# Two-layer hybrid trunk on one core: fp32r sort of tokens, routing beside the first pass, down projection by halves

## What is computed

```
h = rms_norm(x) * gain
g_idx = argmax(softmax(h @ wg + bg))                  # one of 4 groups
e_p, e_idx = top2(softmax(expert logits of that group))  # 2 of its 4 experts
combine = one_hot(expert) * g_p * e_p / sum(e_p)
for e in range(16):
    a = silu(h @ w_gate[e]) * (h @ w_up[e])           # 2048 -> 512
    y += combine[:, e] * (a @ w_down[e])              # 512 -> 2048
x = x + y
```

## Time and profile before

| | us |
|---|---|
| three runs | 1616.9, 1619.32, 1620.0 |
| median | 1619.32 |
| the profiled execution | 1620.66 |
| its span on the engines | 1618.8 |

### The profile page before, as it was taken

How to read it: one execution, slowest core, us unless ns; L and a number is a source line. 1 busy time by engine, 2 the same in 40 slices (tenths; PEclk the granted TensorE clock), 3 DMA queues, 4 the chain that set the end, 5 groups by cost and what they waited for, 6 DMA issues and landing times.

```text
span 1618.8 us, 21643 instructions
## 1 busy us (share of the span) xinstructions
PE 1549.9 (96%) x7394; PEld 1272.5 (79%) x7394; DVE 1388.3 (86%) x1717; ACT 1076.6 (67%) x1286; POOL 11.7 (1%) x23
## 2 busy tenths in 40 slices
PE   5999989988999999999999996899999999999998
PEld 5998786466888888888888885688888888888886
DVE  3389987853799999999999996589999999999998
ACT  4344433053678877878787775478887787787785
POOL 0000000000000000000000000000000000000000
PEclk9999999989999999999999998999999999999999
DMA  8764533433499999999999992179999999999993
GB/s 270 241 208 131 160 128 104 156 142 145 189 380 379 359 350 381 377 339 378 373 353 348 388 348 112 34 287 373 382 358 366 374 377 336 378 376 345 368 373 134
DMA packets 100026, 469.29 MB, mean 290 GB/s; under 512 B 18810, under 2 KB 22220, under 8 KB 50548
## 3 DMA queue, kind: packets, MB, share of 16 engines
q1 hardware_dynamic: 98724, 466.85, 77.9%
q10 hardware_dynamic: 1232, 1.54, 0.3%
HBM read 466.24 MB, written 2.11 MB: 289 GB/s over the span
## 4 chain that ended last, share of the span: by engine, by line
PE 81%; DVE 12%; issue 4%; ACT 2%; DMA 0%; POOL 0%; DVEq 0%; SPq 0%; ACTq 0%; POOLq 0%
PE ps L1514 23%; PE ps L1516 23%; PE ps L1515 23%; DVE split_lo L953 5%; PE ps L1596 3%; PE ps L1803 2%; PE ps L1471 2%; PE ps L1817 1%; DVE cat L953 1%; DVE work L1068 1%; PE ps L1500 1%; ACT split_hi L610 1%; DVE split_lo L957 1%; DVE work L995 1%; DMA x_sb<-in_x 0%
## 5 line engine op out<-in xcount | busy, mean ns | idle before, releaser
L610 ACT ACTIVATE split_hi<-ring 128x1024 fp32r<-128x1024 f32 x856 | 903.6, 1059 | 310.1 <-PE ps L1516 294.2
L953 DVE TENSOR_TENSOR split_lo<-ring,split_hi 128x1024 fp32r<-128x1024 f32 x856 | 1023.0, 1220 | 100.6 <-ACT split_hi L610 70.1
L1514 PE MATMUL ps<-split_hi,cat 128*128 128x512 f32 (+1 forms) x1728 | 680.1, 394 | 8.2 <-DVE cat L953 7.2
L1516 PE MATMUL ps<-split_hi,cat 128*128 128x512 f32 (+1 forms) x1728 | 671.8, 389 | 0.0
L1515 PE MATMUL ps<-split_lo,cat 128*128 128x512 f32 (+1 forms) x1728 | 671.5, 389 | 0.0
L1514 PEld LDWEIGHTS ps<-split_hi,cat 128*128 128x128 f32 x1728 | 325.3, 188 | 82.8 <-issue 17.0
L1516 PEld LDWEIGHTS ps<-split_hi,cat 128*128 128x128 f32 x1728 | 324.9, 188 | 67.5
L1515 PEld LDWEIGHTS ps<-split_lo,cat 128*128 128x128 f32 x1728 | 325.3, 188 | 64.7 <-issue 0.5
L1514 PE MATMUL ps<-cat,split_hi 128*128 128x256 f32 x384 | 112.4, 293 | 11.4 <-DVE split_lo L953 11.4
L1515 PE MATMUL ps<-cat,split_hi 128*128 128x256 f32 x384 | 111.0, 289 | 0.0
L1516 PE MATMUL ps<-cat,split_lo 128*128 128x256 f32 x384 | 110.9, 289 | 0.0
(11 more groups left out here) (181 smaller groups left out, 669.5 us busy)
## 6 DMA issues: line engine op xcount, KB each, us to landing
ring<-in_w_gate SPq DMA_DIRECT2D x128, 1024.0 KB, 5.9
ring<-in_w_up SPq DMA_DIRECT2D x128, 1024.0 KB, 6.2
ring<-in_w_down SPq DMA_DIRECT2D x128, 1024.0 KB, 6.2
ring<-in_w_in_e SPq DMA_DIRECT2D x32, 1024.0 KB, 5.1
ring<-in_w_out_e SPq DMA_DIRECT2D x16, 1024.0 KB, 5.1
ring<-in_pool_w_o SPq DMA_DIRECT2D x4, 1024.0 KB, 8.4
x_sb<-in_x SPq DMA_DIRECT2D x4, 512.0 KB, 6.7
ring<-in_w_in_e SPq DMA_DIRECT2D x8, 256.0 KB, 5.0
```

The lines of the kernel that those rows point to most:

```text
L610: return nc.scalar.activation(out, in_, ACT.Copy, scale=scale)
L953: return tt(dst, full, hi.bitcast(F32), ALU.subtract)
L1514: mm(out, sh, mh, start=start, stop=False, **how)
L1516: return mm(out, sl, mh, start=False, stop=stop, **how)
```

## The change

- **Sort in fp32r.** x is split like a weight: ACT writes `x_parts[0]` (hi) per 512 channels (`hi_of_x`), DVE `x_parts[1]` (lo) (`lo_of_x`), in `cat`, the two token tiles interleaved (a step of 128 bytes between the channels of a group). The one-hot `sort_pick` holds bare ones, in `split_hi`'s slot 3. PE does first all 32 lo matmuls, then all 32 hi, into banks 0 to 7. ACT copies only the first 128 slots to `hgT` at once; `sorted_from(i)` fills `sorted_x` for bank 0 at once and for the others between the splits of the first pass. Unit 3 is split after all banks are sorted (before: ahead of the sort).
- **1/rms** is no longer in the one-hot. Its square is multiplied into the expert weights, and half of it is a fifth column of `comb_now` that the tanh takes as its scale; so `tanh(0)` and `gate(0)` come after the turned picks (unit 19) instead of after unit 10 to 12, in every pass.
- **Routing beside the first pass.** Expert choice, weights, windows and number of passes are cut into eight functions that DVE runs between its splits of units 4 to 15 of the first pass; register reads of the number of passes move behind the first pass on ACT, DVE and PE, the window's read to just before its use.
- **Down by halves.** `down(e)` goes through column halves outside, k inside; a down block is loaded as 2 chunks of k x 1024 columns (4 KB pieces instead of 8 KB).
- **act** is written contiguously by DVE; the transposes read it with a step of four elements.
- **Last pass** is a copy of its own: no slots for a next pass, `y_hi`/`y_lo` of banks 0 and 1 and their first scatters beside the last down; scatters in the order `SCATTER`.
- **Seam.** ACT splits pool units 0 to 2 before the last `y_hi`, DVE units 0 and 1 between its adds, 2 before and 3 after the sum of squares; units 4 to 7 after instead of before the second and fourth add.

```diff
+SCATTER = ((0, 0), (0, 1), (1, 0), (1, 1), (0, 2), (0, 3), (1, 2), (1, 3))
+BANKS_FIRST = {(0, "u"): 2, (1, "g"): 4, (0, "d"): 8}
+        x_parts = [cat[:, at:at + 2 * D].rearrange("p (c t) -> p t c", t=NT) for at in (2 * D, 0)]
+        sort_pick = split_hi[:, SPLITS - 1, 0:NT * 2 * P].rearrange("p (t s) -> p t s", t=NT)
...
+            if kind == "d":
+                half, pair = (j % 4) // 2, j % 2
+                w = a[name][l].rearrange("e (p k) n -> p e k n", k=rows)
+                return w[:, bass.ds(g * EPG + e, 1), 2 * pair:2 * pair + 2, half * HALF:(half + 1) * HALF]
...
+            def hi_of_x(n):
+                cols = slice(n * 512, (n + 1) * 512)
+                copy(x_parts[0][:, :, cols], x_sb[:, :, cols]).then_inc(x_hi, 1)
...
                 turned_x(0, n)
+                hi_of_x(n)
...
-                split(0, 0, 4)
+                split(0, 0, 3)
...
+                def sorted_from(i):
+                    act.wait_ge(m["gather_out"], i + 1)
+                    both = ps[:, i, :].rearrange("p (k s) -> p k s", k=2)
+                    for k in range(2):
+                        last = copy(sorted_x[:, 2 * i + k, :], both[:, k, :], gain_perm[:, l, 2 * i + k:2 * i + k + 1])
+                    last.then_inc(sorted_out, 1)
                 for i in range(8):
+                    if i == 4:
+                        act.wait_ge(gathered, 8 * l + 8)
+                        split(0, 3, 4)
                     act.wait_ge(gathered, 8 * l + i + 1)
...
-                        copy(sorted_x[:, 2 * i + k, :], both[:, k, :], by)
-                        last = copy(hgT[0][:, 2 * i + k, :], both[:, k, 0:P], by)
+                        last = copy(hgT[0][:, 2 * i + k, :], both[:, k, 0:P], gain_perm[:, l, 2 * i + k:2 * i + k + 1])
...
+                    if i == 0:
+                        sorted_from(0)
...
+                    if first_pass:
+                        split(p, 4, 6)
+                        sorted_from(2)
+                        split(p, 6, 8)
+                        sorted_from(3)
+                        split(p, 8, 9)
...
+                        split(p, 9, 11)
+                        sorted_from(1)
+                        for i in range(4):
+                            split(p, 11 + 2 * i, 13 + 2 * i)
+                            sorted_from(4 + i)
...
+                    tanh(0)
...
-                    last = ts(scaled_pick[:, t, :], slot_no, stat[:, 7, t:t + 1], rstd[:, i_norm, t:t + 1], ALU.is_equal, ALU.mult)
+                    last = ts(sort_pick[:, t, :], slot_no, stat[:, 7, t:t + 1], None, ALU.is_equal)
...
                         split(p, 4 + i, 5 + i)
...
+                        if first_pass:
+                            if i == 0: first_choice()
+                            elif i == 2: second_choice()
+                            elif i == 3: group_weight()
+                            elif i == 5: expert_weights()
+                            elif i == 7: combine()
+                            elif i == 8: first_tokens()
+                            elif i == 10: find_windows()
+                            elif i == 11: count_passes()
...
+                    gate(0)
                     times_up(0)
...
+                    if last_pass:
+                        split(p, 84, 89)
+                        turned_lo(EPG - 1)
+                        split(p, 89, 95)
+                        y_lo(p, 0)
+                        split(p, 95, 96)
+                        y_lo(p, 1)
+                        return
...
+                add_y(last_pass, 0)
+                add_y(last_pass, 1)
+                if l == 0:
+                    pool_split(0)
+                add_y(last_pass, 2)
+                add_y(last_pass, 3)
+                if l == 0:
+                    pool_split(1)
+                y_lo(last_pass, 2)
+                y_lo(last_pass, 3)
+                for i in range(4, 8):
+                    add_y(last_pass, i)
...
+                for part in (1, 0):
+                    for i in range(8):
+                        for k in (2 * i, 2 * i + 1):
+                            for t in range(NT):
+                                channels = x_parts[part][:, t, :].rearrange("p (j k) -> p k j", k=KC)[:, k, :]
+                                last = mm(ps[:, i, (k % 2) * SEQ:(k % 2 + 1) * SEQ], channels, sort_pick[:, t, :],
...
-                            last = turn(ps[:, BANK_T, k * P:(k + 1) * P], act[:, k * P:(k + 1) * P])
+                            last = turn(ps[:, BANK_T, k * P:(k + 1) * P], act.rearrange("p (j k) -> p k j", k=FC)[:, k, :])
...
-                        for k in range(FC):
-                            for half in range(2):
-                                between(2 * k + half)
+                        for half in range(2):
+                            for k in range(FC):
+                                between(4 * half + k)
...
+                        elif e == EPG - 1 and last_pass:
+                            down(e, lambda n: scatter(p, n - 6) if n >= 6 else None)
...
+                for i in range(2, 8):
+                    scatter(last_pass, i)
```

More of the change, by code:

```diff
@@ L813, in pool_split @@
                     act.wait_ge(mix_done, 2 * (u // 2 - 1))
+                else:
+                    half_down(act, 0, last_pass, SPLITS + u + 1)
                 for k in range(2):
@@ L966, in wait_job, with lo_of_x @@
                 wait_for_job(dve, name)
+            def lo_of_x(l, n):
+                dve.wait_ge(x_hi, 4 * l + n + 1)
+                cols = slice(n * 512, (n + 1) * 512)
+                low(x_parts[1][:, :, cols], x_sb[:, :, cols], x_parts[0][:, :, cols]).then_inc(x_lo, 1)
             sum_squares(0)
@@ L1275, in moe_dve @@
-                chain(nc.vector.tensor_reduce(col(1), ex_g, X, ALU.add))
-                chain(nc.vector.reciprocal(col(2), col(1)))
-                chain(stt(out=t4a, in0=rank, scalar=float(P), in1=oneh, op0=ALU.is_ge, op1=ALU.mult))
-                chain(nc.vector.tensor_reduce(late, t4a, X, ALU.max))
-                nc.vector.memset(window[:, NG:], float(P))
-                chain(ts(window[:, 0:NG], starts, float(P), None, ALU.min))
-                for t in range(NT):
-                    ts(rank_in[:, t, 0:NG], window[:, 0:NG], -1.0, stat[:, 7, t:t + 1], ALU.mult, ALU.add)
@@ new lines, in group_weight @@
+                def group_weight():
+                    dve.wait_ge(exp_out, 2 * l + 1)
+                    chain(nc.vector.tensor_reduce(col(1), ex_g, X, ALU.add))
+                    chain(nc.vector.reciprocal(col(2), col(1)))
+                    chain(tt(root_sq, rstd[:, i_norm, :], rstd[:, i_norm, :], ALU.mult))
+                    chain(stt(out=t4a, in0=rank, scalar=float(P), in1=oneh, op0=ALU.is_ge, op1=ALU.mult))
+                    chain(nc.vector.tensor_reduce(late, t4a, X, ALU.max))
@@ new lines, in first_tokens, with find_windows @@
+                def first_tokens():
+                    nc.vector.tensor_copy(comb_now[:, :, 0:EPG], comb[:, :, 0:EPG])
+                    ts(comb_now[:, :, EPG:], rstd[:, i_norm, :].unsqueeze(2), 0.5, None, ALU.mult)
+                    for t in range(NT):
+                        last = ts(pick[:, t, :], slot_no[:, 0:P], stat[:, 7, t:t + 1], None, ALU.is_equal)
+                    last.then_inc(m["pick_ready"], 1)
+                    nc.vector.memset(comb[:, :, 2 * NE:], 0.0)
+                def find_windows():
+                    nc.vector.memset(window[:, NG:], float(P))
+                    chain(ts(window[:, 0:NG], starts, float(P), None, ALU.min))
+                    for t in range(NT):
+                        ts(rank_in[:, t, 0:NG], window[:, 0:NG], -1.0, stat[:, 7, t:t + 1], ALU.mult, ALU.add)
+                    ts(rank_in[:, :, NG:2 * NG], col(7).to_broadcast([P, NT, NG]), -float(P), None, ALU.add)
+                    nc.vector.memset(rank_in[:, :, 2 * NG:], -1.0)
+                    chain(nc.vector.tensor_copy(window_i[:, l * NPASS:(l + 1) * NPASS], window))
@@ L1341, in moe_dve, with one_pass @@
                 for i in range(8):
+                    if i == 4:
+                        split(0, 3, 4)
                     dve.wait_ge(m["slots_hi"], i + 1)
-                    two = slice(2 * i, 2 * i + 2)
-                    low(hgT[1][:, two, :], sorted_x[:, two, 0:P], hgT[0][:, two, :]).then_inc(m["gather_out"], 1)
-                def one_pass(p, first_pass=False):
-                    w = dve.value_load(window_i[0:1, bass.ds(p + (l * NPASS + 1), 1)], min_val=0, max_val=P)
+                    both = ps[:, i, :].rearrange("p (k s) -> p k s", k=2)
+                    for k in range(2):
+                        last = low_of(hgT[1][:, 2 * i + k, :], both[:, k, 0:P], gain_perm[:, l, 2 * i + k:2 * i + k + 1],
+                                      hgT[0][:, 2 * i + k, :])
+                    last.then_inc(m["gather_out"], 1)
+                def one_pass(p, first_pass=False, last_pass=False):
```

(1 more changed line is left out.)

256 lines of the change are left out of this document (148 added, 108 removed).

## The result

| | before | after |
|---|---|---|
| median of five runs, us | 1619.32 | 1626.47 |
| lowest, highest | 1616.9, 1620.25 | 1624.96, 1627.8 |
| span of the profiled execution | 1618.8 | 1624.7 |

The ratio is 1.004, with a 95% interval from 1.0029 to 1.0051: slower by 0.4%, some 7 us. The forecast was 1621 in a range of 1609 to 1637, with slower as the likeliest sign (0.48). Range and sign held; the number was 5.5 us too low, and the sign held for a reason that the forecast had put at nothing (see the part on why).

What follows compares the result with a forecast made beforehand. A pass was taken as bound by PE, with DVE close behind. Terms 8.6 + 2 + 0 + 0 - 9.4 - 1 = +0.2 us on the profiled 1620.66 gave 1621, range 1609 to 1637.

Steps and rivals of the forecast that it cites:

- the forecast's own case: The summed forecast, 1621 us, given a chance of 0.36, split in thirds between faster, same and slower.
- (a): Turns of act: every strided transposing load takes 0.22 us and paces PE, +10.5 us, 1631.5; chance 0.30.
- (c): MoE passes: DMA becomes the bound with smaller pieces, a pass takes 140 us, +2.4 x 8, 1640; chance 0.05.
- part 3: Pass boundaries: +1.0 us per layer for register reads after the first pass; steady passes sum 0, bounds -2 and +2.
- Part 1: Sort, both layers: strided weight loads keep fp32r products at 0.22 us; first product -2.3 and -1.1 us.
- rival (b): Sort: fp32r loads aren't slowed, 0.12 us a product, time 1612; chance 0.24 together with the rival on the chain.
- Part 2: First pass: the routing chain between DVE's splits brings unit 20 33.7 us after the first product, loss 6.0 us per layer.
- rival (d): First pass: the routing chain does not displace DVE's splits and costs nothing, time 1609; 0.24 together with (b).
- Part 4: Down projection by halves costs 0; strided turns of act cost 0, bounds 0 and 0.11 us per turn where it shows.
- Part 5: Last pass to pooling, and pooling layer: earlier sums, reordered splits and less slow clock, sum -9.4 us, bounds -4 and -12.
- The pool order: Pooling layer: splits no longer stand before the adds that PE's turns wait for, -3.0 and -0.9 us.
- Part 6: The end: less DVE work after the last matmul, which comes 0.9 us later; net -1 us, bounds 0 and -2.

## Why the prediction was right or wrong

**The number and the sign.** The sum was +0.2 us on the span and +5.9 came, inside the range. That the kernel got slower was luck: the 0.48 for slower came mostly from the upper third of the forecast's own case and from rivals (a) and (c), and both rivals fell (turns read contiguously; down by halves alone). The kernel got slower by a term that part 3 had put at 0; with that one at 0 and all others as measured the span would have become 1.6 us shorter. A steady pass of 139 or more was to speak for (a) or (c); it took 139.1 us and did so for neither reason. Misses also worked against each other: 9.4 us too low in the later passes and the seam, 3.7 us too high elsewhere.

**Part 1, the sort: right.** 0.22 a product was taken, 0.227 measured; -2.3 and -0.9 for -2.3 and -1.1. The argument by the step of the weight load was shown by the contiguous one: 0.120. The rival (b) is out, as loads of fp32r are slowed like those of fp32. The rule of the 16-byte lines that the prediction cites from the Trainium skill, SBUF — State Buffer, section "Door 1: The DMA port swizzle", agrees with these rows, without giving a price. The Trainium skill, TensorE: Matmul & The Clock Gate, section "LDWEIGHTS (loading the stationary operand)", gives a load as its columns divided by 1.2 in ns, 107 for 128; that lies under the 0.120 us at which contiguous products follow, and it says nothing of a step, with which they follow every 0.225.

**Part 2, the chain beside the first pass: right**, 33.7 against 33.3 us to unit 20, and +5.2 for +6.0, so rival (d) is out. The terms given for lo 4 (1.06, four times 0.61, 1.06 and 1.14) add up to 5.7 us, not to the 6.1 that was used; 5.7 us is what the trace has, and it is the 0.4 between the two numbers. What the count left out is the other side of the ledger: the 10 us that DVE is idle under the sort. Nothing had to move.

**Part 3, the later passes: the step that failed.** "`tanh(0)` now stands before ACT's hi 19, so DVE's lo 20 comes some 0.3 us late on PE; the window's register read leaves the pass start, worth about as much. Sum 0". Lo 20 came 1.11 us late in the pass and PE lost 0.75 there, then 0.18 at unit 24; nothing came back at the start of the pass, where the stop before the first scatter is the same (0.46 before, 0.44 after, of starts beyond the usual distance). The direction was right and the term too small, because only the tanh on ACT was counted. Of the 1.11 us that one gave 0.55. Not counted was DVE: `gate(0)`, which used to run ten microseconds ahead of lo 19, now stands together with `times_up(0)` in one piece of 1.55 us, from 728.59 to 730.14, between two splits that PE needs one after the other. The bound of +2 for all passes together was too narrow for 1.17 times six and what the last passes add: 7.5 us. The +1.0 charged per layer for the register reads of the first pass did not show: the 0.4 and 0.5 us of that stage arise by unit 24, as in the other passes, and the row from which it was taken has DVE waiting for ACT's `split_hi`.

**Part 4, halves and turns: right**, 0 for the halves. A stepped turn costs 0.14 us a pass, inside its bounds, and is more than paid for by DVE; rival (a) had the right sign at PE, but a tenth of its price (1.1 us in eight passes against 10.5). Rival (c) was priced too low by its own rows: 365/0.97 is 376 GB/s, not the 385 in its sum, and with it the pass would have become 142.4 instead of 140 us.

**Part 5, the seam: right in mechanism**, -8.4 for -10.3. The band products came at +12.2 for 12; the nine kernels with this seam have 12.2 to 13.4, so this execution lies at the low end. The pool order gave 3.1 of 3.9. The clock gave less than the 2.5 counted: the band products took 9.45 us instead of 10.20 (0.8). Another 0.8 us behind them has no run to itself; before, the clock was at its low level for 3.4 us from 1009.5 on, and in the changed kernel it is not.

**Part 6: right**, -2.4 for -1.9 behind the last down matmul.

## What to carry to other kernels

When an operation is made to depend on a later result, follow everything that stands behind it in order on *each* engine down to the piece of work that the bound engine needs next. The price is how much later that piece begins (1.11 us here, where 0.3 had been counted), and in a loop it is paid every time. Compare each wait with the same wait before: one that stood there already, as ACT's 1.32 us, is no part of the price. Before work is moved out of a stretch, look who will be idle there: the chain fitted under the new sort as it had under the old one. Removing a step from one access can put it into another: the contiguous weight loads gave 5.4 us and the copies behind them took 3.0 back.

## What was not expected of the hardware

- fp32r products of 256 columns whose weight load of 128 columns steps by 128 bytes follow every 0.227 us at 1.2 GHz and every 0.225 at 2.4 GHz; with contiguous loads they follow every 0.213 and 0.120 us. So the pace with the step hardly depends on the clock, and the step adds 0.105 us a product at the full clock but only 0.014 at the low one.
- With a step of 16 bytes the load of the transposes went from 139 to 198 ns of record, but the 18 of a pass (16 of them stepped) cost only 0.14 us of starts.
- An fp32 subtraction on DVE takes 1.22 us for 1024 columns without such a step, so 0.61 for 512; 512 columns take 1.01 us with one input read in steps of 64 bytes, and 1.13 with the output written and one input read in steps of 1 KB. The Trainium skill, VectorE: DVE Perf Modes, section "Mode 1× (REGULAR) — the baseline", gives one result a cycle and says that "fp32, weird strides, PSUM operands — all work"; it has no price for a step, and these rows show one.
